# Attention scores three turns ahead, and the inverse's joins as 64 by 64 products

## The reference

```python
s = jnp.einsum('bnqgrd,bnkgd->bngrqk', qb, kb).astype(jnp.float32) * (D ** -0.5)
...
m = jnp.maximum(jnp.max(s, axis=-1, keepdims=True), sk)
e = jnp.exp(s - m)
p = e / (jnp.sum(e, axis=-1, keepdims=True) + jnp.exp(sk - m))
o = jnp.einsum('bngrqk,bnkgd->bnqgrd', p.astype(vb.dtype), vb)
```

```python
lmat = jnp.where(strict, jnp.einsum('bhncd,bhnsd->bhncs', k_beta, k) * decay, 0.0)
sol = lax.linalg.triangular_solve(eye + lmat, rhs, left_side=True, lower=True,
                                  unit_diagonal=True)
```

## Time and profile before

| | |
|---|---|
| time before, median of 3 runs | 2265.11 us (2264.69 to 2272.47) |
| the profiled execution, its own time | 2264.51 us |
| its span | 2263.2 us |
| mean granted TensorE clock | 0.975 |
| PE busy | 2104.8 us (93%) |
| DVE busy | 1273.8 us (56%) |
| ACT busy | 875.1 us (39%) |
| POOL busy | 893.6 us (39%) |

### The profile page before, as it was taken

One profiled execution on the slowest core, in us unless ns is written; L12 is line 12 of the kernel. 1 busy time (PEld: TensorE's weight loads), 2 busy tenths in 40 slices (PEclk: granted clock), 3 DMA queues, 4 the chain that ended last, 5 costly groups with the idle time before them and its releaser, 6 DMA issues.

```text
span 2263.2 us, 26036 instructions
## 1 busy us (share of the span) xinstructions
PE 2104.8 (93%) x10412; PEld 1702.3 (75%) x10412; DVE 1273.8 (56%) x1943; ACT 875.1 (39%) x1404; POOL 893.6 (39%) x431
## 2 busy tenths in 40 slices
PE   7999999988889899999999899799999998899997
PEld 5888787765556688888787677788788776888786
DVE  5322224665666533222226999887543999877543
ACT  4222233314444543222235375343534385343532
POOL 4444343422113344444343554333344464333342
PEclk9999999998999999999999999899999999899998
DMA  4332323310001232333232222000233222000232
GB/s 148 111 135 94 93 93 121 93 47 28 29 20 56 66 93 94 102 93 98 88 95 83 75 75 66 28 29 20 75 96 100 75 84 65 20 29 20 75 99 78
DMA packets 46183, 169.05 MB, mean 75 GB/s; under 512 B 5232, under 2 KB 6000, under 8 KB 45808
## 3 DMA queue, kind: packets, MB, share of 16 engines
q1 hardware_dynamic: 45344, 165.60, 23.2%
q10 hardware_dynamic: 720, 1.79, 0.2%
HBM read 165.27 MB, written 2.10 MB: 74 GB/s over the span
## 4 chain that ended last, share of the span: by engine, by line
PE 70%; DVE 21%; ACT 6%; issue 2%; DMA 1%; POOL 0%; ACTq 0%; DVEq 0%
PE ps L378 19%; PE ps L380 19%; PE ps L379 19%; DVE cu L1685 4%; DVE acc L1812 2%; PE ps L826 2%; PE ps L584 1%; DVE blk_t L1787 1%; PE ps L405 1%; PE ps L553 1%; DVE outer L1785 1%; DVE st L1534 1%; PE ps L835 1%; PE ps L829 1%; DVE rt L1668 1%
## 5 line engine op out<-in xcount | busy, mean ns | idle before, releaser
L2001 POOL TENSOR_TENSOR wlo<-raw,whi 128x1024 fp32r<-128x1024 f32 x300 | 739.2, 2471 | 946.3 <-ACT whi L903 946.1
L378 PE MATMUL ps<-xh,whi 128*128 128x512 f32 x1600 | 653.0, 408 | 33.8 <-POOL wlo L2001 16.9
L380 PE MATMUL ps<-xh,wlo 128*128 128x512 f32 x1600 | 628.1, 393 | 0.0
L379 PE MATMUL ps<-xl,whi 128*128 128x512 f32 x1600 | 627.8, 392 | 0.0
L903 ACT CAST whi<-raw 128x1024 fp32r<-128x1024 f32 x300 | 312.6, 1044 | 185.5 <-DMA raw<-in_stream 185.5
L378 PEld LDWEIGHTS ps<-xh,whi 128*128 128x128 f32 x1600 | 303.2, 190 | 104.3 <-POOL wlo L2001 16.5
L379 PEld LDWEIGHTS ps<-xl,whi 128*128 128x128 f32 x1600 | 303.6, 190 | 64.2 <-issue 7.0
L380 PEld LDWEIGHTS ps<-xh,wlo 128*128 128x128 f32 x1600 | 302.8, 189 | 64.7
L1685 DVE SCALAR_TENSOR_TENSOR cu<-up,lcols,cu 128x512 f32<-128x512 f32 x180 | 191.7, 1107 | 0.1
L2037 POOL TENSOR_TENSOR cu<-cu,prod 128x512 f32<-128x512 f32 x60 | 85.0, 1416 | 177.7 <-ACT prod L1117 176.5
L1422 DVE TENSOR_TENSOR ml<-mid,mh 128x512 fp32r<-128x512 f32 x42 | 60.4, 1441 | 167.0 <-ACT mh L959 167.0
(11 more groups left out here) (338 smaller groups left out, 3177.4 us busy)
## 6 DMA issues: line engine op xcount, KB each, us to landing
raw<-in_stream SPq DMA_DIRECT2D x300, 512.0 KB, 3.5
w1k<-in_w SPq DMA_DIRECT2D x1, 2048.0 KB, 8.1
w1v<-in_w SPq DMA_DIRECT2D x1, 2048.0 KB, 10.4
outT<-h SPq DMA_DIRECT2D x4, 512.0 KB, 2.7
h<-in_xT ACTq DMA_DIRECT2D x2, 512.0 KB, 7.4
h<-in_xT SPq DMA_DIRECT2D x2, 512.0 KB, 7.8
mats<-in_mats ACTq DMA_DIRECT2D x1, 448.0 KB, 10.4
msk<-in_masks SPq DMA_DIRECT2D x1, 258.0 KB, 3.9
```

Of the source, the lines that this page charges most:

```text
L378: pe.matmul(out, wh, hi, start=first, stop=False)
L379: pe.matmul(out, wh, lo, start=False, stop=False)
L380: return pe.matmul(out, wl, hi, start=False, stop=last)
L2001: pool.tensor_tensor(m.wlo[:, slot, :], m.raw[:, slot, :], m.whi[:, slot, :].bitcast(F32), ALU.subtract).then_inc(s.wlo)
```

## The change

In attention, TensorE's queue becomes `turn(n)`, `score(n + 3)`, `gates(n + 1)`, `apply(n)`, with `score(2)` ahead of the loop. VectorE's becomes the copy of `pt` for turn n, `weights(n + 1)`, `exponents(n + 3)`, with `exponents(2)` ahead of the loop. ScalarE's order stays: it still does the exponentials of turn n+2 after the copy of turn n. The buffers stay two deep, so `score(n + 3)` waits for the exponentials of turn n+1.

In the delta rule, the products L826 and L835 are done only on the 64 by 64 parts that a level uses. At level 1 these are the two diagonal parts of each head, eight products for each direction in place of four. They lie in two opposite corners of the array (rows and columns 0 to 63, and 64 to 127) and go to one bank. At level 2 it is one part for each head and direction; the two directions are interleaved, lie in opposite corners too, and go to different banks. They come after the transposes of both directions, and both directions are released at once.

```diff
--- before.py
+++ after.py
@@ -621,10 +621,11 @@
         gates(0)
         if nsa:
             compressed_turn(0)
+        score(2)
         for n in range(turns):
-            if n < turns - 2:
-                score(n + 2)
             turn(n)
+            if n < turns - 3:
+                score(n + 3)
             gates(n + 1)
             apply(n)
             if nsa and n == 7:
@@ -796,6 +797,26 @@
             heads(lambda n, hs: pe.matmul(X[1][:, hs], m.qkv[:, 4 + n, ts], m.qkv[:, 4 + n, ts], start=True,
                                           stop=True)).then_inc(s.d_kk)
 
+    def half(h, n=0):
+        return slice(n * P + 64 * h, n * P + 64 * h + 64)
+
+    def half_products(out, lhsT, rhs):
+
+        for n in range(DN_H):
+            for h in range(2):
+                ins = pe.matmul(out[half(h), half(h, n)], lhsT[half(h), n, half(h)], rhs[half(h), n, half(h)], start=True,
+                                stop=True)
+        return ins
+
+    def quarter_products(both):
+
+
+        for n in range(DN_H):
+            for out, lhsT, rhs, r, c in both:
+                ins = pe.matmul(out[half(c), half(1 - c, n)], lhsT[half(r), n, half(c)], rhs[half(r), n, half(1 - c)],
+                                start=True, stop=True)
+        return ins
+
     def delta(l):
         nl = len(LEVELS)
 
@@ -823,17 +844,21 @@
                     else:
                         pe.wait_ge(s.d_qd, at + 1)
                         pe.wait_ge(s.d_at, at + 1)
-                    heads(lambda n, hs: pe.matmul(X[0][:, hs], b.AT[:, n, :], b.T[:, n, :], start=True,
-                                                  stop=True)).then_inc(s.d_y)
+                    if lv == 1:
+                        half_products(X[0], b.AT, b.T).then_inc(s.d_y)
                     if lv == 1:
                         heads(lambda n, hs: pe.matmul(X[1][:, hs], m.qkv[:, 4 + n, ts], m.qkv[:, n, ts], start=True,
                                                       stop=True)).then_inc(s.d_qk)
+                if lv > 1:
+                    quarter_products([(X[0], b.AT, b.T, d, 1 - d) for d, at, X, b, ts, t in both]).then_inc(s.d_y, 2)
                 fill(i, f"level{lv}")
                 for d, at, X, b, ts, t in both:
                     pe.wait_ge(s.d_us, level_event(nl, at, lv))
                     pe.wait_ge(s.d_ys, level_event(nl - 1, at, lv))
-                    heads(lambda n, hs: pe.matmul(X[2][:, hs], b.U[:, n, :], b.Y[:, n, :], start=True,
-                                                  stop=True)).then_inc(s.d_uy)
+                    if lv == 1:
+                        half_products(X[2], b.U, b.Y).then_inc(s.d_uy)
+                if lv > 1:
+                    quarter_products([(X[2], b.U, b.Y, 1 - d, 1 - d) for d, at, X, b, ts, t in both]).then_inc(s.d_uy, 2)
                 fill(i, f"join{lv}")
             for d, at, X, b, ts, t in both:
                 heads(lambda n, hs: pe.transpose(X[0][:, hs], m.qkv[:, 4 + n, ts], ident)).then_inc(s.d_ttk)
@@ -1585,19 +1610,20 @@
         exponents(0)
         exponents(1)
         weights(0)
+        exponents(2)
         for n in range(turns):
             pair, i, br = tiles[n]
             at = first + n
             j0, j1 = a_span(call, i)
             w = (j1 - j0) * P
-            if n < turns - 2:
-                exponents(n + 2)
             if at >= 2:
                 dve.wait_ge(s.pv, at - 1)
             dve.wait_ge(s.turned, at + 1)
             dve.tensor_copy(m.pt[:, n % 2, 1, 0:w], ps[:, 6, 0:w]).then_inc(s.pt1)
             if n < turns - 1:
                 weights(n + 1)
+            if n < turns - 3:
+                exponents(n + 3)
 
     def merge(g):
         mixer = g == 0
```

## The result

The changed kernel takes 2229.16 us, the median of four runs (2224.13 to 2232.61), against 2264.9 us before (2256.39 to 2272.47): a ratio of 0.984, 95% interval 0.9821 to 0.986. The forecast was 2230.0. The sum hit, but several of its terms were off, and their errors cancelled: that it came within 1 us is partly luck. The profiled execution took 2232.36 us, with a span of 2231.0.

The account below looks back on a forecast made before the run. TensorE, busy in nearly all of the span, was taken to bound the kernel. The profiled 2264.51 us less 19.5 in attention and 15 in the delta rule gave 2230 us, with a range of 2219 to 2248.

Parts of the forecast that it names:

- The copy of `pt`: Attention: with VectorE's copy first, TensorE's 16.8 us wait before `apply` falls to 2.5, a gain of 14.3 us.
- The gate rows: Attention: TensorE's 11.6 us wait for ScalarE's gate row copies falls to 6.5, gaining 5 us, plus 3 from clock falls.
- What attention loses: Attention: 1.3 us more waiting for compressed weights; `score(3)` and later cost nothing. VectorE's charge was 1.5 us.
- The price of a small product: Delta rule joins, L826 and L835: a 64 by 64 record costs 0.028 us, against 0.111 for a full one.
- The bound of 0.055: Rival, delta rule joins: a record has a floor near 0.055 us, saving 6 us there; 2239 us, chance 0.25.
- the slower one: Rival, L826 and L835 at level 1: small products run one by one at the old pitch; 2277 us, chance 0.04.
- The rival built on it: Rival, level 1: two row halves in one bank run one after the other, pitch 0.055; 2235 us, chance 0.15.
- The change of shape: Delta rule joins: each group that changes the array's shape adds 0.17 us, five in a chunk, 0.85 us.
- What of it lies on the path: Delta rule: of TensorE's shortening, 2.05 us a chunk is passed on; 1.9 taken, eight chunks, 15 us.
- The clock in the delta rule: Delta rule: a lower granted clock beside the 3 us waits was named as a sign of being wrong; no size.
- the likeliest case: The forecast with both parts in full: 2230 us, own range 2222 to 2236, chance 0.43.
- the floor together with a failed attention: Joins at the 0.055 us floor, saving 6 us, with attention saving only 9: said to end above 2254 us.

Follow-up runs that it names:

- att_only: Attention's new order alone, with the joins of the kernel before the change: 2247.48 us, ratio 0.9922 against that kernel.
- delta_only: The 64 by 64 joins of the delta rule alone, with attention as before the change: 2244.94 us, ratio 0.9913 against the kernel before.
- vector_order_only: Changed kernel with VectorE's new order kept, but scores and maximum two turns ahead and TensorE's old attention order: 2280.47 us, ratio 1.007 against before.
- taps_moved: Changed kernel with two VectorE convolution taps per chunk moved from ahead of the keys to past the joins: 2217.28 us, ratio 0.9798 against before.

## Why the prediction was right, and which of its terms were off

**What bounds the kernel, and where the time could come from**: right. Both parts save idle time or work of TensorE, and they add (`att_only`, `delta_only`).

**The copy of `pt`**: right. 2.5 us were to be left, 2.3 are. The copy first alone doesn't do it; the span of `vector_order_only` is 48.6 us longer. The prediction counted on the scores between the transposes and `apply`; that ScalarE waits where VectorE's maximum isn't a turn ahead is what this run added.

**The gate rows**: right. 6.5 us were to be left, 6.2 are, longest 1.3. Behind the wait of the earlier trace rows the clock was 0.60; the same stretch of 711 to 715 us after the change has 1.00.

**What attention loses**: the step that failed. It charged 1.3 us for the wait for the compressed weights. That wait is still 3.9 us, though its longest went from 2.1 to 1.2. It charged 1.5 us for VectorE; the waits for probabilities (L568) are 1.3 us in all. And it said of `score(n + 3)` only what it waits for, not that it stands between two steps of another shape. This term, 6 us, was not in the sum. Idle time fell by 19.6 us: 14.5 (`pt`) and 5.4 (gates), less some tenths elsewhere. Busy time grew by 3.3 us, which is the 6.1 of the changes of shape less 2.8; the 2.8 are what is left for the falls of the clock (3 were forecast). By the clock itself the saving is 9.9 - 6.9 = 3.0. So attention gave 16.3 us, and 19.5 were forecast.

**The price of a small product**: right. 0.028 was taken, 0.029 is measured, for a stationary part, a moving part and two halves of the array all at once. The bound of 0.055, a rival with 0.25, is out, and so is the slower one (its sum used a pitch of 0.107, but the old pitch was 0.111, which makes 35 us instead of 32). The Trainium skill ("TensorEngine Tiling (Array Packing)", Gotcha 1) says that different row tiles can't access the same PSUM bank at once. At level 1 they do by every sign of this trace: L807 with two corners in one bank hands over after 0.61 us, as L816 in two banks does, and its records start in pairs 0.006 to 0.007 us apart, while one corner at a time takes 0.96 instead of 0.68. The rival built on it is out too.

**The change of shape**: mis-sized. 0.17 us for each group was the price of one side. A small group has about 0.14 us in itself (0.61 less 16 x 0.029) and makes the group of full size behind it up to 0.19 longer (1.09 against 0.90). The Trainium skill ("TensorEngine Tiling (Array Packing)", Key Properties) says that changing the tiling mode drains TensorE, and the trace agrees, at both ends of a group.

**What of it lies on the path**: the chain was right, the size not. The path was to pass on 2.05 us at most, because VectorE has no idle time between L1941 and L1949. Counted from the first product of level 1, the second direction's copy starts 13.53 us behind it before (1525.60) and 11.26 after (1465.11, the second of the two in the row at 1464.47): 2.27 earlier, about as forecast. But the lengths behind it aren't fixed. Two taps of the same form went from 4.09 to 2.43 us, and the tap behind them from 0.73 to 1.65. So L1975 starts 17.01 us behind instead of 20.05, and at full clock a chunk saved 2.9 us. TensorE's wait at L854 was to grow; it is gone in the six chunks that had it, and 0.36 us for ScalarE's L1333 stands ahead of L873 (2.1 us in six waits). The first chunk of each layer, which had none, has 1.0 us.

**The clock in the delta rule**: left out of the sum, that is, put at nothing. The prediction named a lower clock there as a sign against it, and it came: 0.79 and 0.64 to 0.65 behind waits where before had 1.00 in two of six. In the four periods its falls moved in both directions: they are 13.4 us shorter in all, 4 x 2.9 = 11.6 by the chain and 1.8 by the clock. Over the whole of the two delta rules it took some 4 to 5 us: they gave 18.4 us in the profiled execution where the chain alone gives 23. The joins alone gave 19.2 (`delta_only`); 15 were forecast. So two errors met here: the chain gave 8 us more than forecast, and the clock took about half of that back.

**The range** held, and so did the likeliest case's own. One sentence on it was wrong: the floor together with a failed attention was said to end above 2254 us, and its own terms give 2264.5 - 9 - 6 = 2249.5. In the profiled execution the saving in attention was forecast 3.2 us too high and that in the delta rule 3.4 too low, and 2.6 us ahead of attention went the other way; the median of the runs lies 3.2 us below that execution. That the sum came so near is luck in that much.

## What to carry to other kernels

When a step is moved in TensorE's queue, count the changes of shape in the new order as well as the waits: one more in a turn cost 0.17 us here, 6 us in all. Small products that lie in opposite corners of the array, given in turn, run two at a time even in one bank (two records each 0.058 us instead of one), but a small group between full ones has 0.14 to 0.33 us of its own, so 16 full records (1.70 us before, 1.08 after) gain much and 8 little (0.17). And a wait of TensorE can cost more than its length: taking 2.5 us out of the 3.1 us wait took the fall of the clock behind it along. That was done by moving work of VectorE that nobody waits for past the result that somebody does.

## What the runs showed of the hardware beyond the forecast

- Groups of 64 by 64 products in one corner at a time went with a granted clock of 0.50 to 0.57 in the 8 us behind a 3.1 us wait, where corners in turn had 1.00, 0.79 and 0.64. The order within one group moved the kernel by 21.7 us, of which its own length explains 7.6.
- Two taps of VectorE with the same form took 1.39, 2.43, 2.60, 3.73 (in `taps_moved`) or 4.09 us. The long ones all had GpSimd's work beside them. A chain through VectorE has no fixed length.
- The fall of the clock behind a 3.1 us wait isn't certain: 1.00 behind two of six before and one of six after. Behind a wait of the same length a chunk takes 38.33, 39.80 or 40.80 us, so a single period tells little of what a change is worth.
